# Low-rank branches of an RWKV-7 layer, computed from the normed rows and the shifted difference instead of from mixed rows

## What is computed

```python
def _rwkv7_mixer(h, shift_prev, S0, mu, w_rkv, w0, w1, w2, a0, a1, a2, g1, g2, ...):
    h_prev = jnp.concatenate([shift_prev[:, None, :], h[:, :-1]], axis=1)
    xx = h_prev - h
    xm = h[:, :, None, :] + xx[:, :, None, :] * mu
    xr, xw, xk, xv, xa, xg = [xm[:, :, i] for i in range(6)]
    r = xr @ w_rkv[0]
    k = xk @ w_rkv[1]
    v = xv @ w_rkv[2]
    w_log = -jax.nn.softplus(-(w0 + jnp.tanh(xw @ w1) @ w2)) - 0.5
    a = jax.nn.sigmoid(a0 + (xa @ a1) @ a2)
    g = jax.nn.sigmoid(xg @ g1) @ g2
    ...
```

## Time and profile before

| | |
|---|---|
| three timed runs | 1759.06 us median, 1754.28 to 1759.59 |
| profiled execution | 1756.67 us |
| its span in the trace | 1754.6 us |
| mean granted TensorE clock | 0.984 of full speed |
| busy share of the span | PE 94%, PEld 90%, DVE 66%, ACT 49%, POOL 42% |
| chain of work that ended last | PE 83%, DVE 8%, ACT 5%, issue 3%, POOL 1% |
| low-rank stage in the span | 409 to 438 us |

### The profile page before, as it was taken

How to read it: one execution, slowest core, us unless ns; L and a number is a source line. 1 busy time by engine, 2 the same in 40 slices (tenths; PEclk the granted TensorE clock), 3 DMA queues, 4 the chain that set the end, 5 groups by cost and what they waited for, 6 DMA issues and landing times.

```text
span 1754.6 us, 37505 instructions
## 1 busy us (share of the span) xinstructions
PE 1654.0 (94%) x14117; PEld 1571.2 (90%) x14117; DVE 1154.9 (66%) x2061; ACT 855.6 (49%) x1604; POOL 739.3 (42%) x815
## 2 busy tenths in 40 slices
PE   6989999996988997999999998999999998999998
PEld 5768999994778997999999877999999976999998
DVE  4786777637478455677764737677774487677753
ACT  3464666423653433366643445466543446556632
POOL 5562666300045110366621445266631763466610
PEclk9999999998999999999999999999999999999999
DMA  7323555453220002455445321355545521555443
GB/s 199 97 74 97 145 155 154 121 154 112 97 96 31 10 4 81 123 154 155 136 133 166 122 60 49 99 162 148 143 132 155 156 82 49 145 144 154 134 134 113
DMA packets 344993, 205.10 MB, mean 117 GB/s; under 512 B 22456, under 2 KB 342312, under 8 KB 344752
## 3 DMA queue, kind: packets, MB, share of 16 engines
q1 hardware_dynamic: 342640, 199.76, 39.7%
q0 software_dynamic: 2080, 3.67, 0.7%
q10 hardware_dynamic: 160, 0.10, 0.0%
HBM read 200.02 MB, written 3.39 MB: 116 GB/s over the span
## 4 chain that ended last, share of the span: by engine, by line
PE 83%; DVE 8%; ACT 5%; issue 3%; POOL 1%; DMA 0%; SPq 0%; DVEq 0%; ACTq 0%; POOLq 0%
PE bank L887 23%; PE bank L888 23%; PE bank L889 23%; PE bank L1239 4%; PE bank L899 2%; ACT hi L1529 1%; DVE lo L2025 1%; ACT LS L1562 1%; PE bank L949 1%; POOL lo L667 1%; PE bank L921 1%; PE bank L1263 1%; DVE xn L2260 1%; ACT PT L1570 1%; PE bank L1178 1%
## 5 line engine op out<-in xcount | busy, mean ns | idle before, releaser
L887 PE MATMUL bank<-XH,hi 128*128 128x320 f32 (+1 forms) x1992 | 628.1, 315 | 10.6 <-DVE lo L2025 3.2
L888 PE MATMUL bank<-XL,hi 128*128 128x320 f32 (+1 forms) x1992 | 618.9, 311 | 0.0
L889 PE MATMUL bank<-XH,lo 128*128 128x320 f32 (+1 forms) x1992 | 618.8, 311 | 0.0
L2025 DVE TENSOR_TENSOR lo<-raw,hi 128x2048 fp32r<-128x2048 f32 (+4 forms) x197 | 418.9, 2127 | 302.6 <-ACT hi L1529 302.6
L887 PEld LDWEIGHTS bank<-XH,hi 128*128 128x128 f32 (+1 forms) x1992 | 375.3, 188 | 24.8 <-issue 7.6
L1529 ACT ACTIVATE hi<-raw 128x2048 fp32r<-128x2048 f32 (+4 forms) x205 | 359.8, 1755 | 75.1 <-PE bank L889 63.5
L888 PEld LDWEIGHTS bank<-XL,hi 128*128 128x128 f32 (+1 forms) x1992 | 375.6, 189 | 1.6 <-issue 0.4
L889 PEld LDWEIGHTS bank<-XH,lo 128*128 128x128 f32 (+1 forms) x1992 | 375.2, 188 | 0.0
L711 POOL TENSOR_TENSOR upad<-upad,rstd 128x128 f32<-128x128 f32 (+1 forms) x176 | 167.5, 971 | 200.1 <-ACT upad L1608 200.1
L887 PE MATMUL bank<-GH,hi 128*128 128x322 f32 x704 | 219.8, 312 | 0.0
L888 PE MATMUL bank<-GL,hi 128*128 128x322 f32 x704 | 218.8, 311 | 0.0
(11 more groups left out here) (378 smaller groups left out, 2353.6 us busy)
## 6 DMA issues: line engine op xcount, KB each, us to landing
raw<-in_f_w_up SPq DMA_DIRECT2D x176, 512.0 KB, 5.0
raw<-in_f_w_down SPq DMA_DIRECT2D x64, 704.0 KB, 4.7
raw<-in_a_w_in SPq DMA_DIRECT2D x12, 1024.0 KB, 5.3
raw<-in_b_w_rkv SPq DMA_DIRECT2D x12, 1024.0 KB, 5.1
raw<-in_a_w_out SPq DMA_DIRECT2D x8, 1024.0 KB, 5.1
raw<-in_b_w_out SPq DMA_DIRECT2D x4, 1024.0 KB, 5.4
raw<-in_c_w_out SPq DMA_DIRECT2D x4, 1024.0 KB, 5.2
raw<-in_a_w_in SPq DMA_DIRECT2D x12, 256.0 KB, 4.6
```

Source lines behind the costliest of these rows:

```text
L887: pe.matmul(out, a, xh(k), start=(start and k == 0), stop=False)
L888: pe.matmul(out, a, xl(k), start=False, stop=False)
L889: last = pe.matmul(out, b, xh(k), start=False, stop=(stop and k == kt - 1))
L2025: dve.tensor_tensor(lo[n % 2][:, 0:w_], raw[n % 2][:, 0:w_], hi[n % 2][:, 0:w_].bitcast(F32), ALU.subtract).then_inc(w_lo, 1)
```

## The change

The mixtures for the low-rank branches are no longer made. Instead `L1` is loaded earlier, behind the last up-projection slab of layer 0's feed-forward layer. POOL multiplies its columns with the branch's `mu` into a new tile `L1X`, at the end of that layer's up projection. PE multiplies `HN` with `L1` and `XX` with `L1X` into the same banks: 32 products of 128 columns each, where before there were 8 of 128 and 16 of 64 columns. The decay and `a` branches share bank 4, the gate is in bank 6. `lora_mix` now counts tiles of `HN` and the finished `XX`. `L2` is loaded where all six loads were before.

```diff
--- before.py
+++ after.py
@@ -379,6 +379,7 @@
         shot = take("shot", [16, 128])
         TK = at("TK", [128, 2, T], F32, rms_at)
         L1 = at("L1", [128, KD, 256], F32, over_s + size([128, KD, T]))
+        L1X = at("L1X", [128, KD, 256], F32, over_s)
         L2 = at("L2", [128, 2, D], F32, over_s - size([128, KD, T]))
         XH2 = at("XH2", [128, KD, T], F32R, over_s - size([128, KD, T]))
         XL2 = at("XL2", [128, KD, T], F32R, over_s)
@@ -469,8 +470,8 @@
         GAIN[norm_final] = ("n_final", 0)
         TILES = ((0, 64), (64, 128), (192, 128))
 
...
         (mx_done, lora_mix, mix_raw, mix_hi, cc_done, decay_done, kk_sq, hs_done, hs_root, hs_inv, fanned, kk_used, gain_done, keys_done, bonus_in, bonus_out) = map(
             sem, "mx_done lora_mix mix_raw mix_hi cc_done decay_done kk_sq hs_done hs_root hs_inv fanned kk_used gain_done keys_done bonus_in bonus_out".split())
         (state_in, rec_begun, rec_pe, rec_act, rec_dve, kb_done, p0_done, iqt_done, y_sq, y_var, y_root, y_normed, y_parts) = map(
@@ -565,13 +566,16 @@
                     sp.wait_ge(w_hi, n - 1)
                     sp.wait_ge(w_lo, n - 1)
 
+            def low_rank_inputs():
+
+                sp.wait_ge(x_done, 8 * xs_of[norm_of[0, "ffn"]] + 8)
+                for c, name in ((slice(0, 64), "b_w1"), (slice(64, 128), "b_a1"), (slice(128, 256), "b_g1")):
+                    sp.dma_start(L1[:, :, c], i_[name][0].rearrange("(k p) n -> p k n", p=128)).then_inc(lora_in, 16)
+
             def low_rank_weights():
 
                 sp.wait_ge(x_done, 8 * xs_of[norm_of[1, "mix"]] + 8)
-                for dst, src in ((L1[:, :, 0:64], i_["b_w1"][0].rearrange("(k p) n -> p k n", p=128)),
-                                 (L1[:, :, 64:128], i_["b_a1"][0].rearrange("(k p) n -> p k n", p=128)),
-                                 (L1[:, :, 128:256], i_["b_g1"][0].rearrange("(k p) n -> p k n", p=128)),
-                                 (L2[0:64, 0, :], i_["b_w2"][0]), (L2[64:128, 0, :], i_["b_a2"][0]), (L2[:, 1, :], i_["b_g2"][0])):
+                for dst, src in ((L2[0:64, 0, :], i_["b_w2"][0]), (L2[64:128, 0, :], i_["b_a2"][0]), (L2[:, 1, :], i_["b_g2"][0])):
                     sp.dma_start(dst, src).then_inc(lora_in, 16)
 
             n = 0
@@ -588,6 +592,8 @@
                                 src = w[:, bass.ds((i * 2 + j) * 128 + h * DFF, 128)].rearrange("(k p) n -> p k n", p=128)
                                 sp.dma_start(dst[:, :, h * 128:h * 128 + 128], src).then_inc(w_raw[(n + j) % 2], 16)
                     n += NF
+                    if layer == 0:
+                        low_rank_inputs()
                 else:
                     wait_free(n)
                     if s.kind == "out" and s.layer == 1 and s.idx == 0:
@@ -723,6 +729,12 @@
                 with pool.Fori(1, NF // 2) as i:
                     for j in range(2):
                         step(i * 2 + j, j, False)
+                if layer == 0:
+                    pool.wait_ge(lora_in, 48)
+                    for c, mu in ((slice(0, 64), 1), (slice(64, 128), 4), (slice(128, 192), 5), (slice(192, 256), 5)):
+                        w_ = V[:, VOFF["b_mu"] + 8 * mu:VOFF["b_mu"] + 8 * mu + 8].rearrange("p (k o) -> p k o", o=1).to_broadcast([128, KD, 64])
+                        ins = pool.tensor_tensor(L1X[:, :, c], L1[:, :, c], w_, ALU.mult)
+                    ins.then_inc(lora_scaled, 1)
                 squares(norm_next(layer), 7 if norm_next(layer) == norm_final else 8)
 
             def pool_rwkv(layer):
@@ -1154,22 +1166,25 @@
 
             def pe_rwkv(layer):
                 s0 = first_slab[layer, "mix"]
-                pe.wait_ge(lora_in, 96)
+                pe.wait_ge(lora_in, 48)
+                pe.wait_ge(lora_scaled, 1)
                 for z in range(2):
-                    for a in range(3):
-                        r_ = (slice(0, 64), slice(64, 128), slice(0, 128))[a]
-                        c_ = (slice(0, 64), slice(64, 128), slice(128, 256))[a]
+                    for src, w_ in ((HN, L1), (XX, L1X)):
                         for k in range(4 * z, 4 * z + 4):
-                            pe.wait_ge(lora_mix, 12 * z + 4 * a + k % 4 + 1)
-                            last = pe.matmul(psum[4 + a][r_, 0:T], L1[:, k, c_], (LW, A, K)[a][:, k, :], start=(k == 0), stop=(k == KD - 1))
-                        if z:
-                            last.then_inc(lora_mid, 1)
+                            pe.wait_ge(lora_mix, 5 * z + (k % 4 + 1 if src is HN else 5))
+                            for y in range(2):
+                                closes = src is XX and k == KD - 1
+                                last = pe.matmul(psum[4 + 2 * y][:, 0:T], w_[:, k, 128 * y:128 * y + 128], src[:, k, :],
+                                                 start=(src is HN and k == 0), stop=closes)
+                                if closes:
+                                    last.then_inc(lora_mid, 1)
                 pe.wait_ge(shift_set, 1)
                 pe.transpose(psum[3][0:16, 0:128], sho[:, :], ident).then_inc(shift_turned, 1)
 
                 def lora_rows(m):
                     if m == 0:
                         pe.wait_ge(shift_out, 1)
+                        pe.wait_ge(lora_in, 96)
                         pe.wait_ge(lora_act, 3)
                     if m >= 2:
                         pe.wait_ge(lora_evac, 3 * m - 3)
@@ -1766,8 +1781,8 @@
 
                 def middle(a):
                     r_ = (slice(0, 64), slice(64, 128), slice(0, 128))[a]
-                    act.wait_ge(lora_mid, a + 1)
-                    act.activation((LTg if a == 2 else LT)[r_, :], psum[4 + a][r_, 0:T], (ACT.Tanh, ACT.Copy, ACT.Sigmoid)[a]
+                    act.wait_ge(lora_mid, 1 + a // 2)
+                    act.activation((LTg if a == 2 else LT)[r_, :], psum[4 + a // 2 * 2][r_, 0:T], (ACT.Tanh, ACT.Copy, ACT.Sigmoid)[a]
                                    ).then_inc(lora_act, 1)
 
                 def lora_rows(m):
@@ -2251,10 +2266,11 @@
                     for k in range(4 * z, 4 * z + 4):
                         ins = dve.scalar_tensor_tensor(out=HN[:, k, :], in0=xT[:, k, :], scalar=gain(GAIN[j], k), in1=rstd[:, :],
                                                        op0=ALU.mult, op1=ALU.mult)
-                    chain(ins)
+                        ins.then_inc(lora_mix, 1)
+                    dve.wait_ge(lora_mix, 5 * z + 4)
                     chain(dve.tensor_tensor(XX[:, k_, 1:T], HN[:, k_, 0:T - 1], HN[:, k_, 1:T], ALU.subtract))
                     dve.tensor_tensor(XX[:, k_, 0], V[:, VOFF["state_b_shift"] + 4 * z:VOFF["state_b_shift"] + 4 * z + 4], HN[:, k_, 0], ALU.subtract)
-                    chain(dve.tensor_scalar(XX[:, k_, 64], HN[:, k_, 64], -1.0, None, ALU.mult))
+                    dve.tensor_scalar(XX[:, k_, 64], HN[:, k_, 64], -1.0, None, ALU.mult).then_inc(lora_mix, 1)
 
                 def mixed(dst, k, mu):
                     return dve.scalar_tensor_tensor(out=dst, in0=XX[:, k, :], scalar=vcol("b_mu", 8 * mu + k),
@@ -2262,9 +2278,7 @@
 
                 for z in range(2):
                     normed(z)
-                    for a, mu in enumerate((1, 4, 5)):
-                        for k in range(4 * z, 4 * z + 4):
-                            mixed((LW, A, K)[a][:, k, :], k, mu).then_inc(lora_mix, 1)
+                dve.wait_ge(lora_mix, 10)
                 dve.tensor_copy(sho[:, 0:8], HN[:, :, 63])
                 dve.tensor_copy(sho[:, 8:16], HN[:, :, T - 1]).then_inc(shift_set, 1)
                 ka = V[:, VOFF["b_k_a"]:VOFF["b_k_a"] + 8]
```

4 lines of the change are left out of this document (2 added, 2 removed).

## The result

The changed kernel took 1764.27 us in the median of 7 runs (1761.27 to 1766.58), the kernel before 1757.03 (1754.28 to 1759.64) beside it. The ratio is 1.0031, 95% interval 1.0021 to 1.0042: 5.5 us slower (3.7 to 7.4). A later series of 11 runs gave 1.0019 (1.0010 to 1.0029). The forecast, 1758.0 and "no change", was wrong.

What follows compares the result with a forecast made beforehand. PE, 83% of the chain, was taken as the bound. Low-rank stage +0.5 us, loads and POOL nothing: profiled 1756.67 + 0.5 = 1757.2 us, median predicted 1758.0, range 1753.5 to 1762.5, no change.

Steps and rivals of the forecast that it cites:

- DVE's gain and PE's bound: Low-rank stage, start of layer 1: DVE 11.1 us earlier, not gained because PE's 64 instructions, 17.2 us, bind the stage.
- some 10 us: Low-rank stage: DVE's expected idle time behind its first two key mixtures, waiting for ACT's high part.
- DVE's time is gained whole: Rival, low-rank stage: products do not bind, second high part could come 11.1 us earlier, total 1747; chance 0.05.
- The stage's size: Low-rank stage, start of layer 1: second high part at 431.7 against 431.23, so +0.5 us.
- The half clock: First low-rank products at 1.2 GHz: 4.06 us long, costing 2.0 us; the other value, 5.0 to 5.4, costing 2.6.
- The loads: L1 loads ahead of layer 0's first down slab: slab lands by 316 instead of 313.7, used at 318.65; no cost.
- POOL's own time: End of layer 0's up projection: four multiplications, 5.2 us, at most some 8, hidden in POOL's 11.24 us of waiting.
- "POOL" beside DVE: End of layer 0's up projection: DVE's subtraction 37% longer, 0.6 us against 0.9 us of slack; no cost.
- its rival: Same place: all of DVE's 4.3 us grow by 37%, PE loses 0.7 us, total 1758.7; chance 0.12.
- The mark that I had set for being wrong: Sign of error: PE shows waits between 318 and 403 us, where it had none before the change.
- Time outside the span: Whole kernel: profiled execution less its trace's span; the prediction gave its change no term.

Runs made afterwards that it cites:

- gate_by_dve: Changed kernel with the gate's 8 mixtures back on DVE, 8 products instead of 16, POOL scaling half as much behind squares 3 and 4: 1753.73 us, ratio 0.9971.
- pe_kept_busy: Changed kernel plus six products of constants into an unused bank, while PE would stand for the reciprocal: ratio 1.0029.
- loads_early: Kernel before with only the three L1 loads moved behind layer 0's last up slab, nothing scaled: ratio 1.0002.
- pool_alone: Kernel before plus four two-tensor POOL multiplications of 128x512 at the end of layer 0's up projection, result unused: ratio 1.0032.
- scale_later: Changed kernel with POOL's four multiplications taken apart, one each behind its squares 3 to 6 of layer 0: ratio 1.0033.
- scale_one_input_timed: Changed kernel with POOL's four two-tensor multiplications written as 24 of a tensor by a per-partition scalar, same place: 1760.44 us, ratio 1.0023.

## Why the prediction was wrong

**DVE's gain and PE's bound: right.** DVE stood 12.13 us behind its first two key mixtures ("some 10 us"), 64 instructions ran without a gap, tanh came when the products were done. The rival "DVE's time is gained whole" is dead, and `gate_by_dve` confirms the account from the other side: with 40 instructions instead of 62 ahead of tanh (bank 4 closes one product before the end), 22 x 0.27 = 5.9 us less, the stage is 5.7 us shorter than the changed kernel's.

**The stage's size: 0.5 forecast, 0.83 measured.** The half clock was there and lasted some 4.8 us (between the two values that I had weighed), 2.3 us by `pe_kept_busy` where I took 2.0. That makes most of the 0.3. In five executions the stage came to 0.3 to 1.3 us over before, by when the clock came back: the first 16 instructions took 6.30 to 7.32 us.

**The loads: right.** Priced at nothing, and nothing by `loads_early`.

**POOL's own time: right, 4.63 against 5.2, and hidden.** It still waited 9.27 us for ACT.

**"POOL" beside DVE: this step failed.** The prediction said that "by the row only this subtraction is known to be" slowed, gave it 37%, and found 0.6 us against 0.9 of slack; its rival applied the 37% to all of DVE's 4.3 us and came to 0.7 us. The mark that I had set for being wrong, a PE wait between 318 and 403, appeared. The direction of the rival was right and its chance, 0.12, far too low; its price was wrong by more than three, 0.7 against 2.4. I had divided the whole subtraction, 2.22 us by 1.62, though POOL's multiplications covered only the start of it. The POOL row of the kernel before that I should have laid beside it:

```profile
318.87 1.97 POOL L711 TENSOR_TENSOR upad<-upad,rstd 128x128 f32<-128x128 f32 x2 [2.34 <-ACT upad L1608]
```

It ends at 320.84, the subtraction starts at 320.10: 0.74 us of overlap cost 0.6. That is not 37% but 80% of the time spent together, DVE all but stopped. The next pair in the same trace says 70%, 0.31 us lost in 0.44:

```profile
325.91 1.67 POOL L711 TENSOR_TENSOR upad<-upad,rstd 128x128 f32<-128x128 f32 x2 [3.02 <-ACT upad L1608]
327.14 1.93 DVE L2025 TENSOR_TENSOR lo<-raw,hi 128x1408 fp32r<-128x1408 f32 x1 [1.67 <-ACT hi L1529]
```

The 5.2 us that the prediction gave POOL, at 0.7 to 0.8, are 3.6 to 4.2 us, and less the 0.9 of slack, 2.7 to 3.3; with the 4.63 measured, 2.3 to 2.8. A PE wait of two to three us could have been read from rows of before; it was 2.4.

The measured pattern, each DVE instruction as long as the POOL instruction beside it, is that of a door that one holds while the other stands. The Trainium skill has it so in "SBUF — State Buffer", section "SBUF: two separate sides": the port pair that DVE and GpSimd share is an exclusive lock, held for the whole instruction. The traces agree for POOL's two-tensor multiplications (1.16 us each in the mean; 0.33, 0.50, 0.55 and 0.55 of DVE became 1.19, 1.22, 1.33 and 1.33). The Trainium skill also says, in the same section, that a DVE instruction with two SBUF inputs contends with a GpSimd instruction that reads SBUF. The traces agree that POOL's multiplications of one tensor contend too, but mostly POOL pays: 2.17 us instead of 0.60 beside a subtraction of 1.61. They don't agree that the pair is held for the whole instruction: while one such multiplication ran from 328.43 to 330.64, DVE began three of two tensors and only one was longer than alone (0.90 instead of 0.55).

**What followed the wait** was in no step: in three profiles of four PE's clock fell to 1.2 GHz at its end or within 1.6 us behind it, 1.5 to 1.7 us more. That it was the wait that brought the fall is argued from the count, three of four against none of ten; no run varied the wait's length.

**Time outside the span** was taken as unchanged. It is 2.67 us in both series of the changed kernel against 2.0, so 0.7 of the slowdown is in no trace. In `pool_alone` it is 2.25.

**The sum**, then: 2.4 to 2.6 (wait) + 3/4 of 1.6 (clock; a share from four profiles only) + 0.8 (stage) + 0.7 (outside) = 5.1 to 5.3 us. The first series says 5.5 (3.7 to 7.4), the second 3.3 (1.8 to 5.1).

**What stays open.** The sum fits the changed kernel's first series, but `scale_later` and `scale_one_input_timed`, which have no wait of 2.4 us, should by it be some 2.4 us (0.9 + 0.8 + 0.7) and 1.0 us (0.8 + 0.2) slower than before, and were 5.8 (3.5 to 8.1) and 4.0 (2.3 to 5.8) by their ratios. So the times don't confirm what the wait is worth; `pool_alone` alone was as slow as the changed kernel. The part of the kernel behind the low-rank stage varies with the clock. The changed kernel's profile, in the second half of layer 1's mixing, and the kernel before in the same part:

```profile
530.53:714.93 184.40, 166.36 (x4086) 159.63 (x4085) 105.97 (x165) 64.47 (x112) 42.11 (x42) 0.94 0.11 34
```

```profile
529.17:710.98 181.81, 163.43 (x4086) 156.80 (x4085) 106.52 (x165) 64.27 (x113) 40.35 (x41) 0.96 0.11 34
```

The same work took 2.6 us longer at 0.94 than at 0.96. But the one-tensor version took 182.01 us there at 0.96; it had lost 3.1 us in the part ahead, from 389 to 448, with the clock low for its first 16 products (7.32 us instead of 6.86). The profiles of all these kernels can be laid side by side, from ACT's second high part to the mean square of the next feed-forward layer. Five with 24 products as before take 303.3 to 305.4 us there, 304.3 in the mean; the kernel before's own, at 303.3, is the shortest. Six with 32 take 304.3 to 308.0, 305.5 in the mean. One source of the spread is seen: right behind the stage a stretch at 1.2 GHz lasted 3.4 us in three of either group and 6.8 us in two of the five and three of the six, and the longer cost 1.3 to 1.8 us. The ranges overlap, so whether the kernels with 32 products meet more low clock than the one before, or whether these are draws, isn't shown; it would bring the two kernels without a wait nearer to their ratios.

## What to carry over

When work is given to POOL "in the shade", look at what DVE does beside it, not at POOL's slack: where the POOL instruction read two tensors, each DVE instruction that met it lasted about one POOL instruction. Divide a slowdown by the time the two really spent together. Multiplying by a per-partition scalar gave DVE back 3.2 - 0.3 = 2.9 us and spared PE the wait, at three and a half times the POOL time; in the time of the whole kernel no gain could be told.

Trading vector work for products pays where it adds none, once PE is what the stage waits for: 16 mixtures went for products of 128 columns in place of as many of 64 (5 us faster), while the gate's 8 mixtures cost 8 additional products, 16 x 0.27 = 4.3 us of PE. Count the instructions, not the columns. A partial undo found the better kernel.

## What was unexpected of the hardware

- Beside DVE, POOL's multiplications of one tensor by a scalar took 2.41 us over 128x512 in the mean, those of two tensors 1.16. With one tensor POOL mostly stands for DVE (128x128: 0.60 alone, 2.17 beside a subtraction), with two it is mostly DVE that stands.
- A cast f32 to fp32r, with one input only, was stopped too: 0.33 to 1.20 us beside the two-tensor multiplications, 0.62 beside the one-tensor ones.
- In the kernel before, products of 64 columns of the two narrow branches ran side by side where both had their inputs: at 1.2 GHz they started at 417.65 and 417.71, then at 418.19 and 418.25, two instructions in the time of one. One branch alone gained nothing by its narrower products.
- A PE wait of 2.4 us inside dense products was followed in three of four executions by a stretch at 1.2 GHz of some 3.4 us. In `pool_alone` it began 1.0 to 1.6 us after PE had resumed (337.80), in the two others with its first products. In ten executions without the wait the clock does not fall between 318 and 403 us.
- Time outside the span differs by program: 2.0 us before, 2.7 changed and in `scale_later`, 2.25 in `pool_alone` and with one tensor, 3.0 in `pe_kept_busy`, 2.0 again in `gate_by_dve`, with the products of constants too. What makes it, no run shows.
